# The second head's operands on the other partition half: four array quadrants in the chunked recurrence, and both heads' products of an inverse level in one row

## The reference, cut to what matters

```python
def step(S, inp):
    r_t, w_t, k_t, v_t, kk_t, a_t = inp
    sa = jnp.einsum('bhvk,bhk->bhv', S, -kk_t)
    S = (S * w_t[:, :, None, :] + sa[..., None] * (kk_t * a_t)[:, :, None, :]
         + v_t[..., None] * k_t[:, :, None, :])
    return S, jnp.einsum('bhvk,bhk->bhv', S, r_t)
```

## Time and profile before

| | |
|---|---|
| median of 3 runs | 1364.66 us |
| the profiled execution, its own time | 1364.41 us |
| its span, first to last instruction | 1362.6 us |
| around the span | 1.8 us |
| granted TensorE clock, mean | 1.000 of full speed |
| busy share of TensorE, VectorE, ScalarE, GpSimd | 97%, 57%, 43%, 28% |
| chain that ended last, share of TensorE | 86% |

### The profile page before, as it was taken

The page is one execution under the profiler, slowest core; times in us unless marked ns, Lnnn a source line. Parts: engine busy times, 40 slices in busy tenths (PEclk is TensorE's granted clock), DMA queues, the critical chain, the costliest instruction groups (busy, mean ns, idle before and its releaser), DMA issues.

```text
span 1362.6 us, 24101 instructions
## 1 busy us (share of the span) xinstructions
PE 1326.2 (97%) x9602; PEld 1065.0 (78%) x9602; DVE 781.0 (57%) x1057; ACT 584.2 (43%) x920; POOL 382.2 (28%) x354
## 2 busy tenths in 40 slices
PE   6999999999999999999999999999999999999999
PEld 5877777878657888888888888776778888888887
DVE  4874556555446766436665448655576663366642
ACT  6564435534234444213444446455554442244421
POOL 3458577657442111000110135532021110011100
PEclk9999999999999999999999999999999999999999
DMA  8100111011312333313333233211023232223331
GB/s 313 47 33 18 52 37 51 19 48 39 141 52 73 93 99 125 101 62 101 100 104 106 82 129 100 78 47 47 12 82 108 92 124 93 77 93 100 123 109 38
DMA packets 30037, 114.10 MB, mean 84 GB/s; under 512 B 3456, under 2 KB 5248, under 8 KB 29184
## 3 DMA queue, kind: packets, MB, share of 16 engines
q1 hardware_dynamic: 29952, 112.89, 25.1%
HBM read 110.78 MB, written 2.10 MB: 83 GB/s over the span
## 4 chain that ended last, share of the span: by engine, by line
PE 86%; DVE 3%; ACT 3%; issue 2%; POOL 1%; DVEq 0%; ACTq 0%; POOLq 0%
PE bank L531 84%; PE bank L820 1%; PE bank L1164 1%; ACT arena L1244 0%; DVE sin_part L2172 0%; DVE cos_part L2199 0%; ACT L1241 0%; ACT L1439 0%; DVE in_lo L1836 0%; PE bank L1048 0%; DVE head_stat L2182 0%; ACT w_hi L1244 0%; PE bank L1071 0%; DVE arena L1825 0%; DVE x L2080 0%
## 5 line engine op out<-in xcount | busy, mean ns | idle before, releaser
L531 PE MATMUL bank<-in_hi,w_hi 128*128 128x512 f32 x704 | 274.9, 390 | 0.9 <-DVE in_lo L1836 0.9
L1244 ACT ACTIVATE w_hi<-ring 128x1024 fp32r<-128x1024 f32 (+1 forms) x144 | 162.3, 1127 | 262.4 <-PE bank L531 262.3
L531 PE MATMUL bank<-in_hi,w_lo 128*128 128x512 f32 x704 | 273.9, 389 | 0.0
L531 PE MATMUL bank<-in_lo,w_hi 128*128 128x512 f32 x704 | 273.9, 389 | 0.0
L2520 POOL TENSOR_TENSOR z_raw<-silu,conv 128x512 f32<-128x512 f32 x40 | 51.5, 1288 | 537.9 <-DVE conv L2123 503.4
L1811 DVE TENSOR_TENSOR w_lo<-ring,w_hi 128x1024 fp32r<-128x1024 f32 (+1 forms) x124 | 165.2, 1332 | 64.5 <-ACT w_hi L1244 64.2
L531 PE MATMUL bank<-arena 64*64 64x64 f32 (+4 forms) x4220 | 175.7, 237 | 12.8 <-issue 3.3
L531 PEld LDWEIGHTS bank<-arena 64*64 64x64 f32 (+2 forms) x4220 | 149.4, 136 | 48.4 <-issue 38.4
L531 PEld LDWEIGHTS bank<-in_hi,w_hi 128*128 128x128 f32 x704 | 132.1, 188 | 29.5 <-DVE in_lo L1836 1.4
L531 PEld LDWEIGHTS bank<-in_lo,w_hi 128*128 128x128 f32 x704 | 132.1, 188 | 27.9 <-issue 0.5
L531 PEld LDWEIGHTS bank<-in_hi,w_lo 128*128 128x128 f32 x704 | 132.1, 188 | 27.5
(11 more groups left out here) (246 smaller groups left out, 2112.7 us busy)
## 6 DMA issues: line engine op xcount, KB each, us to landing
ring<-w_ring SPq DMA_DIRECT2D x119, 512.0 KB, 3.5
ring<-w_ring SPq DMA_DIRECT2D x32, 704.0 KB, 4.1
ring<-w_pairs SPq DMA_DIRECT2D x18, 512.0 KB, 3.5
arena<-w_mem SPq DMA_DIRECT2D x2, 2048.0 KB, 19.7
arena<-w_ring SPq DMA_DIRECT2D x4, 512.0 KB, 4.4
x<-xT SPq DMA_DIRECT2D x1, 2048.0 KB, 9.3
outT<-x SPq DMA_DIRECT2D x8, 256.0 KB, 2.0
mask<-masks SPq DMA_DIRECT2D x1, 1536.0 KB, 6.8
```

What stands on the lines that cost most here:

```text
L531: return nc.tensor.matmul(out, lhsT, rhs, start=first, stop=last, skip_group_check=True)
L1244: return nc.scalar.activation(out, in_, ACT.Copy)
```

## The change

The second head's token-layout operands are kept on the other half wherever that makes four successive products fall on four quadrants. `p ^ hh` is the half. After level 0 `XT` and `Y1` of head 1 are swapped, `X` is not; `W1`, `WA`, the outputs and `yc` of head 1 are swapped too. The transposes of `AR` and of the normalised output become products with `ident64`.

```diff
+        def lora_bank(back):
+            return 7 if back else 1
+        def solve_banks(first, n):
+            return psum[:, 4:6, first:first + n]
...
+            def turned(v, p, hh):
+                return p ^ hh if v else p
+
             def w1_product(j):
-                for hh in range(2):
-                    for c in range(CP):
-                        for p in range(2):
-                            at = (hh * CP + c) * CHUNK
-                            q = mm(bank[7][head(p), at:at + CHUNK], Gm[head(p), hh, c, G_KA, :], Vtok[head(p), c, head(hh)])
+                for c in range(CP):
+                    for p, hh in two(c):
+                        q = mm(bank[hh][head(p ^ hh), c * CHUNK:(c + 1) * CHUNK], Gm[head(p), hh, c, G_KA, :],
+                               Vtok[head(p), c, head(hh)])
...
             def inverse_y(j, v, post):
-                for hh in range(2):
-                    for c in range(CP):
-                        for p in range(2):
-                            at = (hh * CP + c) * CHUNK
-                            q = mm(bank[Y_BANKS[hh]][head(p), at:at + CHUNK], CT[head(p), v * 2 + hh, c, :], X[head(p), hh, c, :])
-                    q.then_inc(sem("cx_mm"), 1)
+                for c in range(CP):
+                    for p, hh in two(c):
+                        q = mm(bank[4 + hh][head(turned(v, p, hh)), c * CHUNK:(c + 1) * CHUNK], CT[head(p), v * 2 + hh, c, :],
+                               X[head(p), hh, c, :])
+                q.then_inc(sem("cx_mm"), 1)
 
             def inverse_d(j, v):
...
+                pe.wait_ge(sem("y1_sb"), LEVELS * j + (v + 1 - LEVELS))
+                for c in range(CP):
+                    for p, hh in two(c):
+                        at = CP * CHUNK + c * CHUNK // 2
+                        half = head(turned(v, p, hh))
+                        o = bank[4 + hh][head(p) if v < LEVELS - 1 else half, at:at + CHUNK // 2].rearrange("p (n b) -> p n b", b=2 << v)
+                        if v < LEVELS - 1:
+                            q = mm(o, XT[half, hh, c, :], blocks(Y1[half, hh, c, :], v, 0))
+                        else:
+                            q = mm(o, Y1[half, hh, c, :], blocks(XT[half, hh, c, :], v, 1))
                 q.then_inc(sem("dx_mm"), 1)
 
             def pq_product(j):
...
+                for c in range(CP):
+                    for p, hh in two(c):
+                        q = mm(bank[4 - 4 * (c // 2) + hh][head(p), c % 2 * P:(c % 2 + 1) * P], XT[head(p ^ hh), hh, c, :],
+                               WA[head(p ^ hh), hh, c, :, :].rearrange("p a d -> p (a d)"))
+                    if c % 2:
+                        q.then_inc(sem("pq_mm"), 1)
...
             def outputs_inside(j):
-                                o = bank[4 + hh][head(p), 2 * P + c * HD:2 * P + (c + 1) * HD]
+                                o = bank[4 + hh][head(p ^ hh), 2 * P + c * HD:2 * P + (c + 1) * HD]
...
+            def removal_to_tokens(j, p):
+                if p == 0:
+                    pe.wait_ge(sem("ar"), 2 * j + 2)
+                    pe.wait_ge(sem("tok_sb"), 3 * j + 2)
+                for c in range(CP):
+                    for hh in range(2):
+                        q = mm(bank[1][head(p ^ hh), c * P + hh * HD:c * P + (hh + 1) * HD], AR[head(hh), 0, 2 * c + p, :],
+                               ident64[head(hh), :])
+                q.then_inc(sem("tok_mm"), 1)
...
             def y_to_features(j):
                 for c in range(CP):
-                    q = nc.tensor.transpose(bank[6][:, c * P:(c + 1) * P], yc[:, c, :, :].rearrange("p h d -> p (h d)"), ident)
+                    for p, hh in two(c):
+                        half = head(p ^ hh)
+                        q = mm(bank[6 + p][head(hh), c * CHUNK:(c + 1) * CHUNK], yc[half, c, hh, :], ident64[half, :])
...
             def step(j, front, back, post, fill):
                 for c in range(1, NCH):
+                    if front and c == 5:
+                        removal_to_tokens(j, 0)
                     if back and c < NCH - 1:
                         chain(j, c)
...
                     if front and c == 3:
-                        gram(j, 1)
+                        gram(j, 1, 0)
...
                     if front and c == 5:
-                        to_tokens(j, 1, pieces(AR[:, 0, :, :]), "ar", 2 * j + 2, "tok_sb", 3 * j + 2)
+                        gram(j, 1, 1)
+                    if front and c == 6:
+                        pe.wait_ge(sem("tok_mm"), 5 * j + 4)
+                        removal_to_tokens(j, 1)
...
             def inverse_y(j, v):
-                for hh in range(2):
-                    act.wait_ge(sem("cx_mm"), 2 * (LEVELS * j + (v + 1 - LEVELS)) + hh - 1)
-                    copy(flat(Y1[:, hh, :, :]), bank[Y_BANKS[hh]][:, hh * CP * CHUNK:(hh + 1) * CP * CHUNK]).then_inc(sem("y1_sb"), 1)
+                act.wait_ge(sem("cx_mm"), LEVELS * j + (v + 1 - LEVELS))
+                copy(Y1.rearrange("p h c t -> p h (c t)"), solve_banks(0, CP * CHUNK)).then_inc(sem("y1_sb"), 1)
...
                 if not last:
-                    V.transpose(flat2(XT), flat2(X)).then_inc(sem("xt_tr"), 1)
+                    V.transpose(flat(XT[:, 0, :, :]), flat(X[:, 0, :, :]))
+                    V.transpose(flat(XT[head(1), 1, :, :]), flat(X[head(0), 1, :, :]))
+                    V.transpose(flat(XT[head(0), 1, :, :]), flat(X[head(1), 1, :, :])).then_inc(sem("xt_tr"), 1)
```

More of the change, by code:

```diff
@@ L61 @@
 KRV_BANKS = 2, 3, 2
-Y_BANKS = 4, 0
 NPAR = 10
@@ L729, in pq_product, with gram @@
                 pe.wait_ge(sem("tok_sb"), 3 * j)
[L730 to L737, removed]
+                for c in range(CP):
[4 more added lines that the diff above has]
+                        q.then_inc(sem("pq_mm"), 1)
+            def gram(j, half, part_of=None):
                 if half == 0:
@@ L743, in gram @@
                     pe.wait_ge(sem("shifted"), 3 * j + 5)
-                else:
+                elif part_of != 1:
                     pe.wait_ge(sem("gr_ev"), 4 * j + 2)
-                for c in range(2 * half, 2 * half + 2):
+                for c in (2 * half, 2 * half + 1) if part_of is None else (2 * half + part_of,):
                     for i, f in enumerate((Kf, Bf)):
@@ L810, in outputs_state @@
                 for hh in range(2):
-                    o = bank[4 + hh][head(c % 2), 2 * P + c // 2 * HD:2 * P + (c // 2 + 1) * HD]
+                    o = bank[4 + hh][head(c % 2 ^ hh), 2 * P + c // 2 * HD:2 * P + (c // 2 + 1) * HD]
                     q = mm(o, Rp[head(hh), c, :], S[head(hh), c, :], False, True)
@@ L838, in step @@
                         pe.wait_ge(sem("b_tok"), j)
-                        pe.wait_ge(sem("tok_sb"), 3 * j)
                     for i in range(2):
-                        mm(bank[i][:, :], ws[head(i), :], lora[head(i), :]).then_inc(sem("lora_mm"), 1)
+                        mm(bank[i * lora_bank(back)][:, :], ws[head(i), :], lora[head(i), :]).then_inc(sem("lora_mm"), 1)
                 if back:
@@ L857, in step @@
                         pe.wait_ge(sem("a_sig"), j + 1)
+                        if back:
+                            pe.wait_ge(sem("w1_sb"), j)
                         for c in range(CP):
@@ L1418, in step @@
                         act.wait_ge(sem("bb"), j)
-                    nc.scalar.activation(aa, bank[1][:, :], ACT.Sigmoid, bias=pcol(j, PA0)).then_inc(sem("a_sig"), 1)
+                    nc.scalar.activation(aa, bank[lora_bank(back)][:, :], ACT.Sigmoid, bias=pcol(j, PA0)).then_inc(sem("a_sig"), 1)
                     if not back:
@@ L1442, in step @@
                     act.wait_ge(sem("w1_mm"), j)
-                    copy(WA[:, :, :, 0, :], bank[7][:, :].rearrange("p (h c d) -> p h c d", h=2, d=HD)).then_inc(sem("w1_sb"), 1)
+                    copy(WA[:, :, :, 0, :], psum[:, 0:2, 0:CP * HD].rearrange("p h (c d) -> p h c d", d=HD)).then_inc(sem("w1_sb"), 1)
                 if post:
@@ L1495, in step @@
                 if back:
-                    for hh in range(2):
-                        act.wait_ge(sem("pq_mm"), 2 * j + (hh - 1))
-                        copy(flat2(PQ[:, hh, :, :, :]), bank[4 + hh][:, :]).then_inc(sem("pq_sb"), 1)
+                    for i in range(2):
+                        act.wait_ge(sem("pq_mm"), 2 * j + (i - 1))
+                        first = 4 - 4 * i
+                        copy(PQ[:, :, 2 * i:2 * i + 2, :, :].rearrange("p h c a d -> p h (c a d)"), psum[:, first:first + 2, 0:2 * P])\
+                            .then_inc(sem("pq_sb"), 1)
                     state(j, 1)
@@ L1932, in inverse_add @@
                 last = v == LEVELS - 1
-                xf = blocks(flat2(XT if last else X), v, int(last))
-                V.tensor_tensor(xf, bank[5][:, 0:T // 2].rearrange("p (n b) -> p n b", b=2 << v), xf, ALU.add)\
+                xf = (XT if last else X).rearrange("p h c (n w b) -> p h (c n) w b", w=2, b=2 << v)[:, :, :, int(last), :]
```

(1 more changed line is left out.)

35 lines of the change are left out of this document (16 added, 19 removed).

## The result

The changed kernel takes **1365.36 us** (median of 20 runs, 1364.23 to 1368.84), the kernel before 1363.85 (20 runs, 1362.43 to 1364.99): ratio 1.0015, 95% interval 1.0008 to 1.0022 (the two medians by themselves give 1.0011). That is inside the 0.2% named as the least that can be told from no change, 0.5 us above the forecast of 1364.9, and the interval lies on the slow side.

A forecast was written before the change was run, and what follows sets the result against it. TensorE's own work, busy 97% of the span, was taken as the bound. Terms -0.1 + 0 - 1.4 + 1.9 = +0.4 on the profiled 1364.41 us gave about 1364.9, range 1361.0 to 1369.5.

The forecast's parts named there:

- TensorE's saving doesn't count: Whole kernel: simple counting gives 33 us saved in six steps, but waits take it back; a steady step sums to 0.0.
- Levels: Level products in a steady step: TensorE stands 1.00 us for the single copy; levels 1 to 3 2.08 us, sum -0.36.
- rival 4: Quadrants sharing a PSUM bank don't run together, so the savings go: 24 us more, 1389; chance 0.04.
- rival 5: Level 0 and the last product serialise, one quadrant after the other: +17 us, 1382; chance 0.04.
- `pq_product` and `gram`: Second half of a step: `pq_product` ends 0.86 us earlier, but `gram` waits for the shifted values; only -0.05 left.
- The chain: Steady step, first transpose to last `outputs_state`: 6.26 us instead of 5.48, +0.77, with removal 1 in the tail.
- the -0.40 of `outputs_inside`: Steady step: `outputs_inside` would end 0.93 us earlier, but the chain waits for `mt_sb` and `rp_sb`; -0.40 remains.
- Stops: Dense stretch of `state_terms` and `outputs_inside`: late instruction packets stop TensorE in all six steps, 5.0 us against 3.1, +1.9.
- Step 6: Last step, without front: +0.6 level 0, -0.69 levels 1 to 3, `pq_product` -0.84, `outputs_inside` -0.75; sum -1.4 us.
- The sum: Whole kernel: -0.1 (step 0) + 0 (steady steps) - 1.4 (step 6) + 1.9 (stops) = +0.4 us; "same" 0.47.

The follow-up runs named there:

- e1: Changed kernel with ScalarE's copy between the level products cut into two halves that products can overlap; 1351.64 us, ratio 0.9918 to the kernel before.
- e6: Changed kernel with one quarter (a 512-column product in step 6) placed between inverse_y and inverse_d of each level; 1347.00 us, ratio 0.9887.
- e0: The changed kernel unchanged, rerun as reference on the chip of some variants; 1366.51 us, ratio 1.0019 to the kernel before.
- e2: Changed kernel with the second block of removal products ahead of the second half of gram(j, 1); 1364.87 us, ratio 1.0007.
- e3: Changed kernel with 16 unread products added in step 0, shifting TensorE's later instructions by 64 places; 1366.47 us, ratio 1.0023.
- e10: e6 with 21 small unread products before gram in steps 1 to 5, making each step whole instruction packets long; 1343.94 us, ratio 0.9854.
- e4: Changed kernel with pq_product reordered, meant to keep only two quadrants busy at a time; 1365.96 us, ratio 1.0018.

## Why the prediction held, and where it did not

**TensorE's saving doesn't count.** Right: 24 us less busy, no time won. e1 and e6 show that the standing in the levels holds most of it (14.9 and 19.5 us under e0, the clock of step 6 included).

**Levels.** Right. Predicted standing 1.00 us, measured 1.03; levels 1 to 3 2.08, measured 2.10, 2.05 and 2.10; level 4 2.55, measured 2.56; `w1_product` with level 0 3.39, measured 3.42 (213.52 to 216.94). Two products in a row on one quadrant cost nothing here: the 64 records of `w1_product` and of `inverse_y` at level 0 start over 1.4 us (1.66 to the modelled end), the 0.47 and 0.94 that were forecast.

**Shared banks (rival 4) and serial products (rival 5).** Refuted. The windows of TensorE alone of the changed kernel (length, busy, clock):

```profile
219.91:220.41 0.50, 0.50 (x33) 1.00 0.00 0
...
248.00:248.92 0.92, 0.92 (x77) 1.00 0.06 18
```

`inverse_y` starts 32 records in 0.48 us and `outputs_inside` 64 in 0.92, 15 ns each, though both row halves write banks 4 and 5. In this kernel the row halves that meet in a bank write different partition halves of it. The rule of the Trainium skill cited with the rival (TensorEngine Tiling (Array Packing), Gotcha 1: PSUM Pressure) does not hold here as it is worded.

**`pq_product` and `gram`.** Right: 0.89 us won and all of it lost to the shifted values.

**The chain.** Predicted 6.26, measured 6.18. With e2's placing over half of the tail's wait came back (0.39 against 0.90), but only 0.33 us of a step. The sum of a steady step counts one 0.05 twice (the -0.40 of `outputs_inside` already has it), which is 0.2 us in all.

**Stops.** Direction right, size and places wrong. The step that failed is "I get stops in all six steps, 0.35 to 1.6 us [...] some 5.0 us against 3.1, +1.9": there are six, but none in step 3 and two in step 5, and 6.8 us in all, +3.7. The mechanism is now shown by e3 (same record, other work), by the starts of the packets, and by e10 (stops nearly gone). Of the added 3.7 part is covered: without its stops each of steps 2, 4 and 5 would be 46.2 (47.54 - 1.34, 46.74 - 0.58, 48.02 - 1.84), 0.4 below step 3 that has none. In steps 1 to 5 together the stops grew by 2.1 us and the steps by 0.5. With the rule of the Trainium skill cited in the prediction (Runtime: NRT & Kernel Launch, Instruction fetch mechanics), that fetch is hidden, this case's trace disagrees: aligning the stream to the borders gave 3.1 us (e10 against e6), and the stops stand in the rows.

**Step 6.** The step that failed is "Sum -1.4" for step 6: it took no account of the clock. Measured 46.75 against 43.50. Taking off the stop of 1.61 and some 1.6 us for each of the two stretches at half clock (e3's step 6 at the full clock is 3.3 us shorter) leaves some 41.9: the part without them is as forecast or better.

**The sum.** Forecast +0.4, by the medians +1.5, by the two profiled executions +3.9. In that pair step 6 is 3.3 us longer and steps 1 to 5 together 0.5, and at the full clock, in e3, step 6 is as long as before by the same bounds (43.28 against 43.30). So nearly all of the 3.9 is the clock, a term that the sum does not have. Two errors met: stops and clock cost more than forecast, and part of the stops lay over waits that were there anyway. So the mechanism of the levels and the chain was right, and that the number came within 0.5 us is in part luck.

## What to carry to other kernels

Doubling the rate of products inside a chain product, copy, product turns TensorE's time into standing unless the copy is cut or other work is put in its place: here a quarter between (0.9887) or halves of the copy (0.9918) gave what the change alone did not (1.0015). Where many small products run at full rate, look for stops of "issue" and count the records between them before explaining them by the work around them. And when TensorE is made faster in a stretch with waits, read the granted clock of what follows.

## What the runs showed of the hardware that was not expected

- TensorE's clock fell to 1.2 GHz inside a kernel that keeps it 95% busy, right after stretches in which it had stood for 2.0 and 1.4 us in all; it cost about 1.6 us each time. It differs by execution: step 6 had two stretches at half clock after, one of twice the length in e0, e2 and e4, and none in e3, where TensorE had stood as long at level 0. What decides it is open.
- In the changed kernel and its variants the stops sit at few numbers of the instruction stream (2439, 4201, 5707, 5963, 7469, 9231, 9481, 9987, 10743), which lie whole packets of about 252 records apart; in the kernel before they are at 2441, 3949 and 8729. Whether a border stops TensorE depends on when its packet starts and when TensorE gets there: TensorE went on 2.15 to 2.7 us behind that start in each stop. The stop varies by execution (step 4: 0.58 after, 1.20 in e0).
- Products of 64 x 16 columns on two quadrants start every 28 ns (41 in 1.14 us), no faster than those of 64 x 64 at 29.
